# The pooling mix of a decoder step: eight fp32 stops become two units of the weights' ring

## The reference, cut to what matters

```
def pool_mix(u, prev, n_prev, w_pool, scale):
    ext = concatenate([prev, u], axis=1)
    cs = cumsum(ext, axis=1) with a zero row ahead
    for g, w in enumerate((2, 4, 8, 16)):
        s = cs[... up to t] - cs[... up to t - w]            # sum over the window
        cnt = minimum(w, n_prev + t + 1)
        outs.append(s / cnt - ext[:, 15:, group g])          # mean minus the token
    d = stack(outs)
    y = einsum('btgc,gcd->btgd', d, w_pool) * scale          # 256 x 256 per group
    return y, ext[:, -15:]
```

## Time and profile before

| | |
|---|---|
| median of three runs | 2173.03 us |
| profiled execution | 2173.22 us |
| its span on the core | 2171.3 us |
| TensorE busy | 2167.5 us, 100% |
| VectorE busy | 1210.6 us, 56% |
| ScalarE busy | 945.7 us, 44% |
| granted TensorE clock | 1.00 |

### The profile page before, as it was taken

The page is one execution under the profiler, slowest core; times in us unless marked ns, Lnnn a source line. Parts: engine busy times, 40 slices in busy tenths (PEclk is TensorE's granted clock), DMA queues, the critical chain, the costliest instruction groups (busy, mean ns, idle before and its releaser), DMA issues.

```text
span 2171.3 us, 43376 instructions
## 1 busy us (share of the span) xinstructions
PE 2167.5 (100%) x18100; PEld 2156.1 (99%) x18100; DVE 1210.6 (56%) x1278; ACT 945.7 (44%) x1054; POOL 23.4 (1%) x35
## 2 busy tenths in 40 slices
PE   9999999999999999999999999999999999999999
PEld 9999999999999999999999999999999999999999
DVE  7776655555555555444466575565555555544443
ACT  7554445434443434443455444454443434433332
POOL 0010000000000000000000010000000000000000
DMA  7655565566565565556565775556565565566664
GB/s 251 207 187 173 169 195 182 170 197 183 178 183 182 181 186 183 182 173 191 184 216 161 223 233 182 183 178 186 178 185 183 174 192 184 174 186 194 194 193 129
DMA packets 218330, 405.31 MB, mean 187 GB/s; under 512 B 15600, under 2 KB 29680, under 8 KB 218064
## 3 DMA queue, kind: packets, MB, share of 16 engines
q1 hardware_dynamic: 201952, 385.22, 57.5%
q10 hardware_dynamic: 16272, 18.55, 2.6%
HBM read 395.86 MB, written 9.93 MB: 187 GB/s over the span
## 4 chain that ended last, share of the span: by engine, by line
PE 100%; DVE 0%; issue 0%; POOL 0%; POOLq 0%
PE ps L622 65%; PE ps L628 32%; PE ps L949 0%; PE ps L695 0%; PE ps L719 0%; PE ps L609 0%; PE ps L709 0%; PE ps L939 0%; PE ps L985 0%; PE ps L929 0%; PE ps L912 0%; PE ps L899 0%; PE ps L671 0%; PE ps L968 0%; PE ps L867 0%; PE ps L752 0%
## 5 line engine op out<-in xcount | busy, mean ns | idle before, releaser
L506 DVE TENSOR_TENSOR wlo<-raw,whi 128x1024 fp32r<-128x1024 f32 (+1 forms) x729 | 882.9, 1225 | 786.9 <-ACT whi L493 785.7
L493 ACT ACTIVATE whi<-raw 128x1024 fp32r<-128x1024 f32 (+1 forms) x729 | 761.1, 1055 | 901.9 <-PE ps L628 880.1
L622 PE MATMUL ps<-xh,whi 128*128 128x264 f32 x3904 | 793.6, 284 | 0.1
L622 PE MATMUL ps<-xl,whi 128*128 128x264 f32 x3904 | 787.2, 283 | 0.0
L622 PEld LDWEIGHTS ps<-xh,whi 128*128 128x128 f32 x3904 | 600.3, 188 | 3.7 <-issue 1.7
L622 PEld LDWEIGHTS ps<-xl,whi 128*128 128x128 f32 x3904 | 599.1, 188 | 0.0
L628 PE MATMUL ps<-xh,wlo 128*128 128x264 f32 x3904 | 556.6, 283 | 0.0
L628 PEld LDWEIGHTS ps<-xh,wlo 128*128 128x128 f32 x3904 | 504.4, 188 | 0.0
L622 PE MATMUL ps<-hh,whi 128*128 128x264 f32 x1920 | 387.1, 283 | 0.0
L622 PE MATMUL ps<-hl,whi 128*128 128x264 f32 x1920 | 387.0, 283 | 0.0
L622 PEld LDWEIGHTS ps<-hh,whi 128*128 128x128 f32 x1920 | 294.4, 188 | 0.1
(11 more groups left out here) (246 smaller groups left out, 514.2 us busy)
## 6 DMA issues: line engine op xcount, KB each, us to landing
raw<-in_w_gate SPq DMA_DIRECT2D x176, 512.0 KB, 4.2
raw<-in_w_up SPq DMA_DIRECT2D x176, 512.0 KB, 4.2
raw<-in_w_down SPq DMA_DIRECT2D x176, 512.0 KB, 3.7
raw<-in_w_in_even SPq DMA_DIRECT2D x71, 512.0 KB, 4.6
raw<-in_w_in_odd SPq DMA_DIRECT2D x66, 512.0 KB, 4.3
raw<-in_w_out_odd SPq DMA_DIRECT2D x32, 512.0 KB, 4.2
raw<-in_w_out_even SPq DMA_DIRECT2D x16, 512.0 KB, 4.7
raw<-in_w_out_even SPq DMA_DIRECT2D x32, 256.0 KB, 4.1
```

Source lines behind the costliest of these rows:

```text
L493: ins = act.activation(dst, src, ACT.Copy)
L506: ins = dve.tensor_tensor(dst, src, hi.bitcast(F32), ALU.subtract)
L622: pe.matmul(ps[:, bank + t, 0:T], whi[:, s, c:c + P], r[k0 + kk], start=first and kk == 0 and m == 0, stop=False)
```

## The change

The pooling weights become two units of the ring. `ODD_UNITS` lists the 68 steps that result; the two mixing units stand at steps 58 and 61, so all units from step 58 on move by one step and those from 60 on by two. A mixing unit holds `w_pool` of two groups, 1 KB pieces instead of 2 KB. It is split like any other, and TensorE does its 24 products in three terms, into four PSUM banks (4 to 7) instead of one. Those banks belong to the state updates until step 56, so the first mixing unit waits for `sg_ok`, `go_ok` and `ostd`.

The means are now split too: ScalarE copies `dmix` to a high part at the same steps 42, 47, 51 and 55 at which VectorE forms it, and VectorE subtracts at the step after. VectorE's next mean waits for that (`dm_lo`) instead of for TensorE's stop. The parts of groups 0 and 1 lie in unused chunks of `hh` and `hl`, those of groups 2 and 3 where `wpool` was. The transposes `out_T` and what follows them move from steps 60, 62, 64 to 63, 64, 66. The DMA of `w_pool` on ScalarE's queue at step 40 is gone. A semaphore of GpSimd's first memset is merged with another.

```diff
-U_OUT_O = U_ODD + 8 * IN_UNITS + 2
+U_OUT_O = U_ODD + 8 * IN_UNITS + 2 + 2
-ODD_FIRST = (0, 8, 10, 18, 26, 34, 42, 50, 58)
+ODD_MIX = (58, 61)
+def odd_units():
+    order = [(q, j) for q, col in enumerate(ODD_COLS) for j in range(IN_UNITS if col is not None else 2)]
+    for j, s in enumerate(ODD_MIX):
+        order.insert(s, (None, j))
+    return order
-POOL_AT = tuple(range(44, 60, 2))
+MEANS_AT = (42, 47, 51, 55)
...
 SyncE
+                    if q is None:
+                        sp.dma_start(slot.rearrange("p (k n) -> p k n", k=4),
+                                     a["w_pool"][0, 2 * j:2 * j + 2].rearrange("g (k p) n -> p (g k) n", p=P)
+                                     ).then_inc(raw_full[n % RING], 16)
...
 TensorE
-            def pool_mix(c):
-                g, m = divmod(c, 2)
-                pe.wait_ge(dmix_ok, g + 1)
-                pe.wait_ge(d_wp, 16)
-                pe.wait_ge(pml, c) if c else pe.wait_ge(go_ok, 4)
-                for k in range(2):
-                    mm = pe.matmul(ps[:, 4, 0:T], wpool[:, 2 * g + k, m * P:(m + 1) * P], dmix[:, k, :],
-                                   start=k == 0, stop=k == 1)
-                mm.then_inc(pm_ps, 1)
+            def pool_mix(n, j):
+                pe.wait_ge(lo_done, n + 1)
+                pe.wait_ge(dm_lo, 2 * j + 2)
+                if j:
+                    pe.wait_ge(pml, 4)
+                else:
+                    pe.wait_ge(go_ok, 4)
+                    pe.wait_ge(sg_ok, 16)
+                    pe.wait_ge(ostd, 1)
+                hi, lo = (z[:, n % RING, :].rearrange("p (k n) -> p k n", k=4) for z in (whi, wlo))
+                for t in range(4):
+                    g, m = t // 2, t % 2
+                    dh, dl = mix_in(2 * j + g)
+                    for x_, (w, r) in enumerate(((hi, dh), (hi, dl), (lo, dh))):
+                        for k in range(2):
+                            mm = pe.matmul(ps[:, 4 + t, 0:T], w[:, 2 * g + k, m * P:(m + 1) * P], r[k],
+                                           start=x_ == 0 and k == 0, stop=x_ == 2 and k == 1)
+                    mm.then_inc(units_done if t == 3 else pm_ps, 1)
-                    if s in (60, 64):
-                        out_T((s - 60) // 4)
-                    if s in POOL_AT:
-                        pool_mix(POOL_AT.index(s))
+                    if s in (63, 66):
+                        out_T((s - 63) // 3)
...
 ScalarE
-                if s == 40:
-                    act.wait_ge(d_go[0], 32)
-                    act.wait_ge(d_go[1], 32)
-                    act.wait_ge(go_ps, 4)
-                    act.dma_start(wpool[:, :, :], a["w_pool"][0].rearrange("g (k p) n -> p (g k) n", p=P)).then_inc(d_wp, 16)
+                for g in range(4):
+                    if s == MEANS_AT[g]:
+                        if g == 2:
+                            act.wait_ge(d_go[0], 32)
+                            act.wait_ge(d_go[1], 32)
+                            act.wait_ge(go_ps, 4)
+                        act.wait_ge(dmix_ok, g + 1)
+                        for k in range(2):
+                            ins = act.activation(mix_in(g)[0][k], dmix[:, k, :], ACT.Copy)
+                        ins.then_inc(dm_hi, 1)
-                if s in POOL_AT:
-                    c = POOL_AT.index(s)
-                    act.wait_ge(pm_ps, c + 1)
-                    act.activation(hh_c[8 + c], ps[:, 4, 0:T], ACT.Copy,
-                                   scale=vec[:, V_PSC + c:V_PSC + c + 1]).then_inc(pmh, 1)
+                if s in ODD_MIX:
+                    for t in range(4):
+                        c = 4 * ODD_MIX.index(s) + t
+                        if t < 3:
+                            act.wait_ge(pm_ps, 3 * (c // 4) + t + 1)
+                        else:
+                            act.wait_ge(units_done, U_ODD + s + 1)
+                        act.activation(hh_c[8 + c], ps[:, 4 + t, 0:T], ACT.Copy,
+                                       scale=vec[:, V_PSC + c:V_PSC + c + 1]).then_inc(pmh, 1)
...
 VectorE
                 if g:
-                    dve.wait_ge(pm_ps, 2 * g)
+                    dve.wait_ge(dm_lo, g)
+            def mix_low(g):
+                hi, lo = mix_in(g)
+                dve.wait_ge(dm_hi, g + 1)
+                dve.wait_ge(dmix_ok, g + 1)
+                dve.wait_ge(wu_ok, 1)
+                for k in range(2):
+                    ins = dve.tensor_tensor(lo[k], dmix[:, k, :], hi[k].bitcast(F32), ALU.subtract)
+                ins.then_inc(dm_lo, 1)
-                if s in (42, 47, 51, 55):
-                    window_means((42, 47, 51, 55).index(s))
+                if s in MEANS_AT:
+                    window_means(MEANS_AT.index(s))
+                if s - 1 in MEANS_AT:
+                    mix_low(MEANS_AT.index(s - 1))
```

More of the change, by code:

```diff
@@ L253, in decoder_step @@
         attS = put("attS", [P, 8, P], after("st"))
-        wpool = put("wpool", [P, 8, 256], after("k2t"))
+        dmix_b = put("dmix_b", [P, 7, T], after("k2t"), F32R)
+        assert after("dmix_b") <= after("attS")
         sgl_a = put("sgl", [P, 4, 2, 256], after("attS"))
@@ L266, in sgl, with mix_in @@
             return sgl_a[:, k, :, :] if k < 4 else sgl_b[:, k - 4, :, :]
+        def mix_in(g):
+            if g < 2:
+                return [[z[12 + 2 * g + k] for k in range(2)] for z in (hh_c, hl_c)]
+            b = [dmix_b[:, k, :] for k in range(7)] + [dmix_c[:, :]]
+            return [b[4 * z + 2 * g - 4:4 * z + 2 * g - 2] for z in range(2)]
         d0 = put("d0", [P, 4, T], after("sgl"))
@@ L391, in decoder_step @@
         pml = sem("pml")
-        d_wp = sem("d_wp")
+        dm_hi = sem("dm_hi")
+        dm_lo = sem("dm_lo")
         d_pst = sem("d_pst")
@@ L577, in _ @@
             n = U_ODD
[L578 to L582, removed]
+            for q, j in ODD_UNITS:
+                base = None if q is None else ODD_COLS[q]
+                if base is not None:
+                    load(n, w_odd, 2 * P * j, base)
+                else:
+                    sp.wait_ge(lo_done, n - RING + 1)
+                    slot = raw[:, n % RING, :]
+                    if q is None:
[3 more added lines that the diff above has]
+                    else:
+                        sp.dma_start(slot.rearrange("p (k n) -> p k n", k=8),
                                      w_odd[8 * P * j:8 * P * (j + 1), ZR:ZR + P].rearrange("(k p) n -> p k n", p=P)
                                      ).then_inc(raw_full[n % RING], 16)
[L585 to L589, removed]
+                n += 1
             assert n == U_OUT_O
@@ L972, in _ @@
             tiles_before = 3 * EVEN_GROUPS
[L973 to L977, removed]
+            for s, (q, j) in enumerate(ODD_UNITS):
                     n = U_ODD + s
-                    if col is None:
+                    if q is None:
+                        pool_mix(n, j)
+                    elif ODD_COLS[q] is None:
                         pe.wait_ge(lo_done, n + 1)
@@ L988, in _ @@
                     else:
+                        G = G_ODD + q
                         if q == 0:
@@ L1019, in _ @@
                             dec_out(b)
-                    if s in (60, 64):
-                        out_T((s - 60) // 4)
-                    if s in POOL_AT:
-                        pool_mix(POOL_AT.index(s))
-                if col is not None:
-                    tiles_before += 3
+                    if s in (63, 66):
+                        out_T((s - 63) // 3)
+                    if j == IN_UNITS - 1:
+                        tiles_before += 3
             out_proj(U_OUT_O, G_OUT_O, OUT_O_ORDER, tiles_before, False)
@@ L1372, in _ @@
                 for half in range(2):
-                    if s == (63, 65)[half]:
+                    if s == (65, 67)[half]:
                         act.wait_ge(oc_ok, half + 1)
@@ L1732, in _ @@
             take.tiles = 3 * EVEN_GROUPS
-            group_end = {s0 + (IN_UNITS if c is not None else 2) - 1: q for q, (c, s0) in enumerate(zip(ODD_COLS, ODD_FIRST))}
+            group_end = {s: q for s, (q, j) in enumerate(ODD_UNITS) if q is not None and j == (IN_UNITS if ODD_COLS[q] is not None else 2) - 1}
             def gla_states(h):
@@ L1896, in _ @@
                     dec_state(s - 40)
-                if s in (42, 47, 51, 55):
-                    window_means((42, 47, 51, 55).index(s))
[L1899 to L1903, removed]
+                if s in MEANS_AT:
+                    window_means(MEANS_AT.index(s))
+                if s - 1 in MEANS_AT:
+                    mix_low(MEANS_AT.index(s - 1))
+                if s in ODD_MIX:
+                    for t in range(4):
+                        c = 4 * ODD_MIX.index(s) + t
+                        dve.wait_ge(pmh, c + 1)
+                        dve.scalar_tensor_tensor(hl_c[8 + c], ps[:, 4 + t, 0:T], vec[:, V_PSC + c:V_PSC + c + 1],
```

(5 more changed lines are left out.)

18 lines of the change are left out of this document (11 added, 7 removed).

## The result

The changed kernel took 2179.80 us in the median of seven runs (2179.03 to 2180.97), the kernel before 2173.00 us beside it (2172.75 to 2173.14). The ratio is 1.0031 with a 95% interval of 1.0022 to 1.0041: slower by 6.8 us. The profiled execution has a span of 2178.2 us, 6.9 more than before.

What follows compares the result with a forecast made beforehand. TensorE, busy for the whole span, was taken as the bound, so its new waits add in full. Terms -1.7 + 1.8 + 0.2 + 4.6 = +4.9 us gave 2178.0 us, 0.23% slower, range 2174.8 to 2182.5.

Steps and rivals of the forecast that it cites:

- trade: On TensorE, eight fp32 pooling stops removed, two mixing units added: a gain of 1.3 to 2.1 us, taken as 1.7.
- A: Step 44: TensorE's second half of `dec_out` waits for VectorE's late state update; 1.8 us, between 1.2 and 2.7.
- B: Step 50: TensorE's unit 50 waits for VectorE's evacuation of the first tile; 0.2 us, none to 1.2.
- C: Step 58: the first mixing unit waits for `ostd`, behind the late store of state 14; 4.6 us, 3.0 to 6.0.
- clock behind C: TensorE's clock falling to half rate after wait C; the forecast sum held nothing for it.
- rival 3: Wait C lets TensorE's clock fall, losing 2.7 us more: +7.6 in all, 2180.7 us; chance 0.16.
- Unit 61: Waits for evacuation of unit 58's tiles; three TensorE units, 8.7 us, were to cover it, so it was costed at nothing.

Runs made afterwards that it cites:

- The fourth experiment: Changed kernel with ScalarE's transfers put before its wait for the means only in the last of the four steps (group 3): 2177.82 us, ratio 1.0019.
- the kernel with both moves: Changed kernel with ScalarE's transfers before its waits for the means in all four steps, and mixing units at 59 and 62: 2171.93 us, ratio 0.9996.
- Transfers first: Changed kernel with ScalarE's transfers put before its wait for the means in all four steps: 2175.18 us, ratio 1.0010.
- only the first two steps moved: Changed kernel with ScalarE's transfers before its wait for the means only for groups 0 and 1: 2176.92 us, ratio 1.0018.

## Why the prediction was right, and which sizes were off

The forecast was 2178.0 us, and 2179.80 was measured, inside the range, slower as the likeliest outcome had it. It even lies in the forecast's own range of 2176.2 to 2180.2, and that is partly luck: a term of 2.5 us that the sum had at nothing fell into its width. I measure each term on TensorE from the outer product of step 43 to the second transposes, 77.21 us before and 84.38 after, so +7.17:

| term | predicted | measured | how |
|---|---|---|---|
| trade | -1.7 | -1.27 | 5.81 less 7.08 |
| A | +1.8 | +1.22 | 1.65 less 0.43 |
| B | +0.2 | +1.10 | 1.27 less 0.24, and 0.07 in the next pair |
| C | +4.6 | +3.66 | 3.90 less 0.24 |
| clock behind C | 0 | +2.50 | 5.38 less 2.88 |
| sum | +4.9 | +7.21 | |

- **The trade** came out at the alternative that the prediction named and did not take: the 0.20 us by which the stops behind `dec_out` looked dearer belonged to the end of `dec_out` and stayed.
- **A** is right in mechanism and at the low end that the prediction gave for a quick state load.
- **B** is the high end that it gave for a late state load, and a late load it was, not by its landing (8.0 us, before 8.7) but by its issue, 1.72 us later. I mis-sized it because I took the queue of step 44 as undisturbed by A.
- **C** is right step by step. Counted from the outer product of step 55 at 1277.76, the store went at +3.28 (predicted +2.75, VectorE came 0.6 us late, for a reason that the last section shows), the copy to `dS` at +6.65 (+7.35, since the store landed in 3.3 us and not 4.6), `ostd` was there at +10.73 (+11.4), and TensorE at +7.21 (+7.2). The fourth experiment adds what the count had missed: a second path through ScalarE's own order, behind the mean and a split. It brought the copy to `dS` at +5.00, only 1.65 us before the path through the landing did, so an early store could win no more of C than that.
- **The clock** is the step that failed. The prediction set it up as rival 3 in place of the forecast, at 0.16, because the gap was "a few microseconds in a dense stream". It came with the forecast: 2.50 us against the 2.7 that the rival gave. Without it the measured terms come to 4.71, the forecast's 4.9 almost exactly, but by errors that cancel: the trade and B came out higher by 0.43 and 0.90, A and C lower by 0.58 and 0.94. By the rule of the page named above, TensorE: Matmul & The Clock Gate in the Trainium skill, it would have been a term of the sum from the start.
- **Unit 61** showed no wait, as predicted; a wait of 0.5 us came only when both units moved by one.

The same terms account for the experiments. On that stretch the kernel with both moves is at -0.91 us: -1.27 and one gap of 0.31. Transfers first is at +1.30: -1.27, a wait of 2.52 and 0.08 in the next pair. With only the first two steps moved it is +4.36: -1.27, a wait of 4.08 and about 1.6 of clock. The other four kernels come out within 0.1 us in the same way.

## What to carry to other kernels

A copy that waits for another engine should be queued behind the transfers of its step, not ahead of them: the copy was not urgent, and the stores and loads behind it were. A wait of an engine that was busy all the time can cost the clock behind it too; here 3.66 us of waiting brought 2.50 us more, 2.0 us brought 1.6 in one kernel and 2.5 us nothing in the profile of another, and even useless products in the gap won 1.9 us. Before a consumer is put on a chain (here one with two table loads), count the chain from its last input, and put the consumer one unit further back: with the transfers first, that move hid the 2.4 us which reordering had left.

## What the runs showed of the hardware that was not expected

A pair of VectorE's subtractions with both inputs in SBUF took 1.96 us beside GpSimd's window sums, where the same pair took 0.77 us without them. Timeline of VectorE after, the pair at two steps and a low part between them:

```profile
1239.28 0.77 DVE L1823 TENSOR_TENSOR hl<-dmix,hh 128x264 fp32r<-128x264 f32 x2
...
1258.93 1.21 DVE L527 TENSOR_TENSOR wlo<-raw,whi 128x1024 fp32r<-128x1024 f32 x1
...
1271.96 1.96 DVE L1823 TENSOR_TENSOR dmix_b<-dmix,dmix_b 128x264 fp32r<-128x264 f32 x2
```

Timeline of GpSimd after:

```profile
1259.10 1.99 POOL L2033 TENSOR_TENSOR tree<-ext 128x540 f32<-128x540 f32 x1 [22.91 <-DVE pst L1857]
...
1269.09 4.54 POOL L2033 TENSOR_TENSOR tree<-tree 128x536 f32<-128x536 f32 x3
```

The pair at 1271.96 lies almost wholly within GpSimd's sums and took 1.96 us; that at 1239.28 does not and took 0.77. Before, a low part at 1272.63 took 2.24 us against the 1.22 of its group. SBUF — State Buffer in the Trainium skill, section "Who interferes with whom", says that such an operation with both inputs in SBUF contends with GpSimd's reads, and these rows agree. Not every such operation was slow beside the sums: the low part at 1258.93 took its usual 1.21 us, and there it was GpSimd's sum that took 1.99 us, against 1.09 for a sum of the same shape at 1233.94, while VectorE was idle (times of GpSimd are rough in the profile).

The slow pair lay on the path to wait C. In the changed kernel VectorE has no idle time from 1270.02 to the end of the fourth mean at 1281.00. Its update of step 55 began 1.05 us behind its outer product, where it was 0.45 us before, though its state had landed by 1278.1. So, of the 1.19 us by which the pair was slow, some 0.6 us came through to the fourth mean, the store of state 14 and `ostd`. This is read from the trace; no run moved the pair. The prediction counted these subtractions at nothing as work.
